# Latent attention on one core: rotation by repeated rows, one table of inverse roots, queries left unnormed until the exponential

## The reference

```python
def pool_mixer(u, pool_w, pool_scale):
    ...
    for g, w in enumerate(POOL_WINDOWS):
        lo = jnp.clip(t - w // 2, 0, S - 1)
        hi = jnp.clip(t + w - 1 - w // 2, 0, S - 1)
        sums = cs[:, hi + 1, g] - cs[:, lo, g]
        cnt = (hi - lo + 1).astype(jnp.float32)[None, :, None]
        outs.append(sums / cnt - ug[:, :, g])
    d = jnp.stack(outs, axis=2).astype(u.dtype)
    y = jnp.einsum('bsgc,gcd->bsgd', d, pool_w).reshape(B, S, POOL_WIDTH)
    return y * pool_scale

def mla_mixer(c_q, c_kv, k_r, q_lora_g, w_uq, kv_lora_g, w_ukv, q_g, k_g):
    q = (rms_norm(c_q, q_lora_g) @ w_uq).reshape(B, S, MLA_HEADS, MLA_QK)
    kv = (rms_norm(c_kv, kv_lora_g) @ w_ukv).reshape(B, S, MLA_HEADS, MLA_NOPE + MLA_V)
    k_nope, v = kv[..., :MLA_NOPE], kv[..., MLA_NOPE:]
    k = jnp.concatenate([k_nope, jnp.broadcast_to(k_r[:, :, None, :], (B, S, MLA_HEADS, MLA_ROPE))], axis=-1)
    q = rms_norm(q, q_g)
    k = rms_norm(k, k_g)
    q = jnp.concatenate([q[..., :MLA_NOPE], rotary(q[..., MLA_NOPE:], pos)], axis=-1)
    k = jnp.concatenate([k[..., :MLA_NOPE], rotary(k[..., MLA_NOPE:], pos)], axis=-1)
    o = blocked_attention(q, k, v)   # softmax over 512 keys, 128 queries at a time
```

## Time and profile before

| | |
|---|---|
| Time, three runs | 3940.98 us median (3920.44 to 3941.12) |
| Profiled execution: its time, its span | 3940.72 us, 3938.9 us |
| TensorE's granted clock, mean | 0.941 |
| PE / DVE / ACT / POOL busy | 93% / 53% / 32% / 3% |
| Length of the changed part: end of `pool[1]` to first matmul of `mix_out[0]` | 150.4 to 396.3 us |

### The profile page before, as it was taken

The page is one execution under the profiler, slowest core; times in us unless marked ns, Lnnn a source line. Parts: engine busy times, 40 slices in busy tenths (PEclk is TensorE's granted clock), DMA queues, the critical chain, the costliest instruction groups (busy, mean ns, idle before and its releaser), DMA issues.

```text
span 3938.9 us, 42380 instructions
## 1 busy us (share of the span) xinstructions
PE 3648.7 (93%) x17470; PEld 2846.9 (72%) x17470; DVE 2083.8 (53%) x3851; ACT 1256.4 (32%) x2098; POOL 111.9 (3%) x216
## 2 busy tenths in 40 slices
PE   7767999999998989999999998999999899889999
PEld 6422767888786768887798566788888786567886
DVE  5665457885665448884314655433333425644444
ACT  4334333333445333333311213332322312224332
POOL 0000000000113000000000000000000000000000
PEclk9878999999999999999999867999999999779999
DMA  5200214552221214552411011122221321112231
GB/s 166 84 0 0 71 48 150 171 171 96 82 70 35 75 43 160 172 171 89 150 54 54 9 46 43 43 65 65 63 67 39 136 65 36 37 46 78 93 97 64
DMA packets 213565, 315.39 MB, mean 80 GB/s; under 512 B 5241, under 2 KB 162555, under 8 KB 212093
## 3 DMA queue, kind: packets, MB, share of 16 engines
q1 hardware_dynamic: 197564, 241.39, 19.0%
q0 software_dynamic: 15808, 71.31, 5.2%
HBM read 300.09 MB, written 14.49 MB: 80 GB/s over the span
## 4 chain that ended last, share of the span: by engine, by line
PE 80%; DVE 13%; ACT 4%; issue 2%; DMA 1%; POOL 0%; SPq 0%; DVEq 0%; POOLq 0%; ACTq 0%
PE ps L94 79%; DVE t L115 5%; ACT t L100 4%; DVE t L107 4%; DVE t L111 1%; PE ps L97 1%; DVE ps L107 1%; DVE ps L115 1%; DVE ps L112 0%; DVE t L112 0%; DVE t L121 0%; DVE t L118 0%; DMA t<-gates_away 0%; DVE t L125 0%; DMA t<-in_mem 0%
## 5 line engine op out<-in xcount | busy, mean ns | idle before, releaser
L94 PE MATMUL ps<-t,t 128*128 128x512 f32 (+7 forms) x16990 | 3557.8, 373 | 258.8 <-DVE t L107 99.9
L94 PEld LDWEIGHTS ps<-t,t 128*128 128x128 f32 (+4 forms) x16990 | 2782.5, 192 | 1008.7 <-issue 223.6
L100 ACT ACTIVATE t<-t 128x1024 fp32r<-128x1024 f32 (+7 forms) x1207 | 853.7, 740 | 1275.9 <-PE ps L94 900.4
L107 DVE TENSOR_TENSOR t<-t,t 128x1024 fp32r<-128x1024 f32 (+5 forms) x884 | 779.1, 906 | 719.0 <-ACT t L100 704.1
L100 ACT ACTIVATE t<-ps 128x512 f32<-128x512 f32 (+6 forms) x481 | 244.4, 530 | 1134.0 <-PE ps L94 1037.5
L115 DVE SCALAR_TENSOR_TENSOR t<-t,t,t 128x256 f32<-128x256 f32 (+4 forms) x951 | 448.4, 535 | 7.6 <-ACT t L100 1.2
L107 DVE TENSOR_TENSOR t<-ps,t 128x512 f32<-128x512 f32 (+4 forms) x308 | 198.1, 663 | 300.7 <-PE ps L94 216.1
L115 DVE SCALAR_TENSOR_TENSOR t<-ps,t,t 128x512 f32<-128x512 f32 (+1 forms) x220 | 133.6, 658 | 279.3 <-PE ps L94 279.1
L118 DVE COPY t<-ps 128x256 f32<-128x256 f32 (+3 forms) x173 | 78.9, 483 | 273.8 <-PE ps L94 255.4
L100 ACT ACTIVATE t<-ps,t 128x512 f32<-128x512 f32 (+3 forms) x153 | 93.7, 617 | 192.5 <-PE ps L94 120.1
L112 DVE TENSOR_SCALAR ps<-ps 128x512 f32<-128x512 f32 (+2 forms) x61 | 39.5, 661 | 110.8 <-ACT t L100 110.8
(11 more groups left out here) (30 smaller groups left out, 304.1 us busy)
## 6 DMA issues: line engine op xcount, KB each, us to landing
t<-in_w_ff SPq DMA_DIRECT2D x64, 1024.0 KB, 7.6
t<-in_w_mlp SPq DMA_DIRECT2D x64, 1024.0 KB, 5.2
t<-in_ada_w POOLq DMA_DIRECT2D x48, 1024.0 KB, 5.7
t<-in_w_in SPq DMA_DIRECT2D x30, 1024.0 KB, 5.3
t<-in_w_qkv_o SPq DMA_DIRECT2D x12, 1024.0 KB, 5.2
t<-in_w_mem_kv SPq DMA_DIRECT2D x8, 1024.0 KB, 6.2
t<-in_w_mem_q SPq DMA_DIRECT2D x8, 1024.0 KB, 5.1
t<-in_w_mem_o SPq DMA_DIRECT2D x8, 1024.0 KB, 5.1
```

What stands on the lines that cost most here:

```text
L94: return Issued(self, self.e and self.e.matmul(o, l, r, start=start, stop=stop, skip_group_check=True))
L100: return Issued(self, self.e and self.e.activation(o, i, f, **kw))
L107: return Issued(self, self.e and self.e.tensor_tensor(o, a, b, op))
```

## The change

Nothing outside the part described above changes but tables: the constants grow by 208 columns (`sel`), and the up-projections are laid out anew on the host.

- Up-projection of queries: the matrix has 128 columns per head: 64 plain, the 32 rotated ones, and the same 32 with halves exchanged. One DVE pass out of PSUM multiplies by gains and by `E0.QROPE` (ones, cosines, sines) and gives `E0.QF`, 128 rows for each head; even heads have the plain rows first, odd heads last. The inverse root of the query is not applied.
- Keys: the shared rotated rows are turned once (a 32-row matmul, three small DVE passes) and copied by four DMAs into both repeated places of all heads of `E0.KX`; ACT copies the plain rows. A score is then one 128-row product.
- Roots: squares of the 12 projection tiles go as stationary operand against 16 columns of `sel`; the sums of 8 queries and 8 keys gather in one bank, [128 tokens, 4x16]. One Ln, one Exp, one Newton step give `E0.RQ` for all. The query's root enters as the per-token scale of the score's exponential (`RQS`, and `NRQ` for the maximum). The key's root is spread over partitions by four 128x128 matmuls against the identity (`key_roots(h)`) and multiplied into `E0.KX` (`keys(h)`), two heads ahead.
- Attention: scores in three banks (0, 1, 2), transposes in 3 and 4. Values for two heads together, on every second turn, with the matmuls of the two heads alternating: one writes rows 0 to 63 of bank 5, the other rows 64 to 127 of bank 7.
- Pools: ACT copies the projected groups out of PSUM into padded rows `E0.R`; the shifted sums, the product and the difference are on GpSimd. `pool_mix` moves into the turns 2 to 5 of attention, its evictions into turns 3 to 6.
- SP: `E0.QROPE` is loaded into a staging buffer, then SP waits for the turned key rows and for `pool[1]`, starts the four copies, and waits for the last query tile before it loads on.

The diff, cut to its core (removed lines are those of the functions above):

```diff
+    E0.M, pt = ar([128, 2, 8, S], R), ar.at
+    E0.WQ, E0.INV = place([128, 2, 1024], F, D1S + 8192), place([128, 4, S], F, D1S + 24576)
+    E0.PT, E0.V = [ar([128, 4, S]) for _ in range(2)], ar([128, 4, 512])
+    E0.R, E0.U, E0.U2 = [ar([128, S + 32]) for _ in range(4)], ar([128, S + 32]), ar([128, S + 32])
+    E0.PW, E0.RQ, E0.RQS, E0.NRQ = ar([128, 4, 128]), ar([128, 64]), ar([128, 64]), ar([128, 64])
+    ar = Area(HRbase := DYN, D1S)
+    E0.QF, E0.KX = ar([128, 8, S]), ar([128, 8, S])
+    spare = U.pool[1].i % 2
+    E0.SB = [place([128, 4, S], F, HLbase[spare] + 8192 * i) for i in range(2)]
+    E0.QROPE = place([128, 2, S], F, STGbase[spare])
...
+        opening(7)
+        pe.wait_ge("krg")
+        pe.matmul(P[7][64:96, :], cst("perm96")[64:96, 64:96], E0.KR[64:96, :], True, True).then_inc("krot")
+        free[7] = [("krt",)]
         feature(U.pool[1], HR1, normed("mix0"))
...
+        def norm_sum(x):
+            kind, n = latent[x]
+            sel = cst("sel")[:, 16 * (n if kind == "q" else 8 + n):][:, 0:16]
+            pe.wait_ge("psq", x)
+            for i in range(4):
+                ins = pe.matmul(P[6][:, 16 * i:16 * i + 16], squares[x % 4][:, 128 * i:128 * i + 128], sel, False, x == 11)
+            ins.then_inc("psum", x)
...
+        pe.wait_ge("krsq")
+        for i in range(4):
+            pe.matmul(P[6][:, 16 * i:16 * i + 16], E0.KSQ[64:96, 128 * i:128 * i + 128], cst("sel")[64:96, 192:208], i == 0, False)
+        for x, (kind, n) in enumerate(latent):
+            bk = latent_banks[x % 6]
+            opening(bk)
+            if kind == "k":
+                pe.matmul(P[bk][:, :], E0.WKV[:, 128 * n:128 * n + 128], E0.CKV[:, :], True, True).then_inc("pk", n)
+                free[bk] = [("psq", x), ("kx", n, 0), ("kx", n, 1)]
+            else:
+                for kk in range(2):
+                    ins = pe.matmul(P[bk][:, :], E0.WQ[:, kk, 128 * n:128 * n + 128], E0.CQ[:, kk, :], kk == 0, kk == 1)
+                ins.then_inc("pq", n)
+                free[bk] = [("psq", x), ("qf", n)]
+            if x > 1:
+                norm_sum(x - 2)
+        norm_sum(10)
+        norm_sum(11)
+        free[6] = [("rs", "mlar")]
+        for i in range(4):
+            bk = latent_banks[i]
+            opening(bk)
+            pe.matmul(P[bk][:, :], E0.CKV[:, 128 * i:128 * i + 128], E0.WKV[:, 512:1024], True, True).then_inc("val", i)
+            free[bk] = [("val_out", i)]
...
+        def key_roots(h):
+
+            opening(6)
+            pe.wait_ge("rs", "mlar")
+            for i in range(4):
+                ins = pe.matmul(P[6][:, 128 * i:128 * i + 128], E0.RQ[:, 16 * i + 8 + h:16 * i + 9 + h].broadcast_to([128, 128]),
+                                cst("ident"), i == 0, i == 3)
+            ins.then_inc("rkb", h)
+            free[6] = [("kf", h)]
...
+            free[6] = [("mixed", m)]
...
+        def transposes(h, kt):
+            bk = 3 + kt % 2
+            opening(bk)
+            for q in range(4):
+                pe.wait_ge("prob", h, q)
+                ins = pe.transpose(P[bk][:, 128 * q:128 * q + 128], E0.SB[h % 2][:, q, 128 * kt:128 * kt + 128], cst("ident"))
+            ins.then_inc("tp", "mla", h, kt)
+            free[bk] = [("pt", h, kt)]
...
+        for h in range(-1, 9):
+            for q in range(4):
+                g = h + 1
+                if g < 8:
+                    bk = (4 * g + q) % 3
+                    opening(bk)
+                    pe.wait_ge("kf", g)
+                    pe.matmul(P[bk][:, :], E0.QF[:, g, 128 * q:128 * q + 128], E0.KX[:, g, :], True, True).then_inc("qk", "mla", g, q)
+                    free[bk] = [("sfree", "mla", g, q)]
+                if q == 0 and h > 0 and h % 2 == 0:
+                    j = h // 2 - 1
+                    opening(5)
+                    opening(7)
+                    for kt in range(4):
+                        for a in range(2):
+                            pe.wait_ge("pt", 2 * j + a, kt)
+                            ins = pe.matmul(P[5 + 2 * a][64 * a:64 * a + 64, :], E0.V[:, kt, 64 * (2 * j + a):64 * (2 * j + a) + 64],
+                                            E0.PT[a][:, kt, :], kt == 0, kt == 3)
+                    ins.then_inc("pv", "mla", j)
+                    free[5], free[7] = [("ol", "mla", j, 0)], [("ol", "mla", j, 1)]
+                if q == 2 and 0 <= h < 6:
+                    key_roots(h + 2)
+                if 0 <= h < 8 and q > 0:
+                    transposes(h, q - 1)
+                if q == 3 and 2 <= h < 6:
+                    pool_mix(h - 2)
+            if 0 <= h < 8:
+                transposes(h, 3)
...
+
+        def pool_in(u):
+            act.wait_ge("pads")
+            for t in u.tiles:
+                act.wait_ge(*ready(u, t))
+                act.activation(E0.R[t.m][:, 16:16 + S], t.views[0].ps, ACT.Copy).then_inc("ev", u.n, t.m, 0)
+
+        pool_in(U.pool[0])
+        pool_in(U.pool[1])
+        for x, (kind, n) in enumerate(latent):
+            ps = P[latent_banks[x % 6]][:, :]
+            act.wait_ge("pk" if kind == "k" else "pq", n)
+            act.wait_ge(*(("psum", x - 4) if x >= 4 else ("hss", "ql", 1) if x < 2 else ("nlo", "mix0", 7, 0)))
+            act.activation(squares[x % 4][:, :], ps, ACT.Square).then_inc("psq", x)
+            if kind == "k":
+                    act.activation(E0.KX[64 * a:64 * a + 64, 2 * n + a, :], ps[64 * a:64 * a + 64, :], ACT.Copy).then_inc("kx", n, a)
+        act.wait_ge("psum", 11)
+        act.activation(E0.RQ[:, :], P[6][:, 0:64], ACT.Ln, bias=EP[:, 0:1], scale=1.0 / 96).then_inc("ln", "mlar")
+        act.wait_ge("ln", "mlar")
+        act.activation(E0.RQ[:, :], E0.RQ[:, :], ACT.Exp, scale=-0.5).then_inc("guess", "mlar")
...
+        def copies(h, kt):
+            act.wait_ge("tp", "mla", h, kt)
+            if h >= 2:
+                act.wait_ge("pv", "mla", h // 2 - 1)
+            act.activation(E0.PT[h % 2][:, kt, :], P[3 + kt % 2][:, :], ACT.Copy).then_inc("pt", h, kt)
...
+                    act.wait_ge("max", "mla", g, q)
+                    act.activation(E0.SB[g % 2][:, q, :], P[(4 * g + q) % 3][:, :], ACT.Exp, bias=st[:, 1:2],
+                                   scale=E0.RQS[:, 16 * q + g:16 * q + g + 1], accum_out=st[:, 2:3]).then_inc("sfree", "mla", g, q)
...
+        for x, (kind, n) in enumerate(latent):
+            if kind == "q":
+                dve.wait_ge("pq", n)
+                dve.wait_ge("psq", x)
+                dve.scalar_tensor_tensor(E0.QF[:, n, :], P[latent_banks[x % 6]][:, :], vec("mlaq_g", n % 2), E0.QROPE[:, n % 2, :],
+                                         ALU.mult, ALU.mult).then_inc("qf", n)
+        newton([("mlar", P[6][:, 0:64], E0.RQ[:, :])], 1.0 / 96)
+        dve.wait_ge("rs", "mlar")
+        dve.tensor_scalar(E0.RQS[:, :], E0.RQ[:, :], 96 ** -0.5, None, ALU.mult).then_inc("rqs")
+        dve.tensor_scalar(E0.NRQ[:, :], E0.RQ[:, :], -(96 ** -0.5), None, ALU.mult).then_inc("nrq")
+
+        def keys(h):
+            dve.wait_ge("kx", h // 2, h % 2)
+            dve.wait_ge("kr_in")
+            dve.wait_ge("rkb", h)
+            dve.scalar_tensor_tensor(E0.KX[:, h, :], E0.KX[:, h, :], vec("mlak_g", h % 2), P[6][:, :], ALU.mult, ALU.mult).then_inc("kf", h)
+
...
+                    dve.tensor_tensor(st[:, 1:2], st[:, 0:1], E0.NRQ[:, 16 * q + g:16 * q + g + 1], ALU.mult).then_inc("max", "mla", g, q)
...
+        pl.wait_ge("mla_weights")
+        for m in range(4):
+            pl.wait_ge("ev", U.pool[m // 2].n, m, 0)
+            a, b, c = E0.R[m], E0.U, E0.U2
+            lo, hi, step = 8, 8 + S + 15, 1
+            pl.wait_ge()
+            pl.tensor_tensor(b[:, lo:hi], a[:, lo - 1:hi - 1], a[:, lo:hi], ALU.add).then_inc()
...
+            pl.wait_ge()
+            pl.tensor_tensor(c[:, 16:16 + S], b[:, 16:16 + S], E0.INV[:, m, :], ALU.mult).then_inc()
+            pl.wait_ge()
+            pl.tensor_tensor(a[:, 16:16 + S], c[:, 16:16 + S], a[:, 16:16 + S], ALU.subtract).then_inc("pooled", m)
...
+        sp.wait_ge("lo", U.pool[1].i, 1)
+        sp.dma_start(E0.QROPE[:, :, :], A["qrope"]).then_inc(s_rope, "qrope")
+        sp.wait_ge("krr")
+        for y, r in enumerate((64, 96, 0, 32)):
+            src = E0.KRR[64:96, :].rearrange("p (a t) -> p a t", a=1).broadcast_to([32, 4, S])
+            ins = sp.dma_start(E0.KX[r:r + 32, y // 2::2, :], src)
...
+        sp.wait_ge("qf", 7)
```

342 lines of the change are left out of this document (143 added, 199 removed).

## The result

| | before | after |
|---|---|---|
| Time, median | 3938.18 us (3920.44 to 3941.12, four runs) | 3808.16 us (3806.64 to 3832.28, four runs) |
| Ratio of after to before | | 0.9694, 95% interval 0.9653 to 0.9735 |
| Profiled execution: its time, its span | 3940.72, 3938.9 us | 3806.64, 3804.9 us |
| Granted clock, mean | 0.941 | 0.952 |

Faster by 3.1%, as forecast: 3808 for 3810 us, inside the range.

What follows compares the result with a forecast made beforehand. TensorE, busy 93% of 3938.9 us, was taken as the bound, with its waits in the changed part to be won; its re-added time line starts the output projection 131 us earlier, so 3940.7 us becomes 3810 us, range 3785 to 3843.

Steps and rivals of the forecast that it cites:

- Step 1: Before the projections: turning the shared key rows once, two TensorE instructions, 0.9 us, to 151.3 us.
- Step 2: Projections and roots: TensorE the bound, small instructions at 0.12 us, 32.6 us in sum, to 183.9 us.
- Step 3: Projections to attention: spreading of roots, DVE's product and two value copies behind the value tiles; first score at 187.1 us.
- Step 4 and 5: Attention turns: 7.2 us without values; 11.3 us with values, ACT the bound, value pair 3.6 us side by side.
- Step 6: Pools in the turns: TensorE 0.86 us more where it waits for ACT anyway; DVE 0.75 more; +0.75 us.
- Step 7: Attention's sum: warming up 5.4, turns 64.6, last transposes and values 8.1 us, from 187.1 to 265.2 us.
- Beside it: Work beside TensorE: GpSimd passes 1.9 to 2.8 us, ending at 176 to 192; DMAs covered; scale column taken at zero.
- (a): Rival, value products: the array's halves take turns, +3.4 us in each of four pairs, 3823 us; chance 0.17.
- (b): Rival, clock: half clock in the projections' part, up to 3843 us; in the turns too, 50 more; chance 0.09.
- (c): Rival, turns: hand-overs as long again, or DVE late by another 2 us each turn, 3826 to 3835 us; chance 0.12.
- (d): Rival, attention: heads still run one after the other, 27.3 us a turn, 3922 us; chance 0.04.
- (e): Rival, pools on GpSimd: each us they end after 215 delays the end by one; 3971 us at 13 a pass; chance 0.03.

Runs made afterwards that it cites:

- e4: Changed kernel with each of the 48 small sum products (16 columns) done twice, the second into an unread bank; 3831.12 us.
- e11: Changed kernel with one extra 512-column float32 product for each of the twelve projection tiles, into an unread bank; 3821.16 us.
- e5: Changed kernel with the 18 pool passes moved back from GpSimd to DVE; 3805.07 us.
- e7: Changed kernel with the four pool products and their evictions moved from the attention turns into the projections; 3813.13 us.
- e8: Changed kernel with five contraction steps of the output projection's first tile pair put into the gaps at the end of attention; 3803.07 us.
- e2: Changed kernel with every GpSimd pool pass done three times, 54 passes in place of 18; 3820.60 us (one execution).
- e1: Changed kernel with the value instructions of a pair's two heads one head after the other instead of alternating; 3824.41 us.
- e3: Changed kernel with every GpSimd pool pass done five times, 90 passes in place of 18; 3861.99 us (one execution).

## Why the prediction was right, point by point

The mechanism was right: TensorE's own work in this order, nearly without waits, sets the time. That the time came within 2 us of the forecast is in part luck. With the turning of the key rows (0.9 us) the changed part takes 116.8 us, 2.0 more than the forecast's 114.8, and inside it terms are off by up to 2 us either way; what lies ahead of it was 1.5 us shorter in this execution than before, and what lies behind it 3.4.

- Step 1. The turning of the shared key rows stands in front of `pool[1]` and its 0.9 us went into the stretch before; the projections begin at 149.8 us, not 151.3. From run to run this start lies between 149.8 and 152.6 us, so that these 1.5 us are luck.
- Step 2, projections and roots. 32.6 us to 183.9 predicted; 149.8 to 182.2 us measured, 32.4, with TensorE busy all the time. A small product with 16 columns costs 0.112 us, against 0.12 from the row of one column; e4 gives the same. Of the bounds 0.10 and 0.43 the first was the near one; by it the sum would have been 2 us less, and not the 10 that the prediction names, which is what all these products cost together. That TensorE is the bound is shown by e11, and e5 shows that DVE is not.
- Step 3. From the first spreading of roots (182.2) to the first score (185.5) 3.3 us, for 3.2.
- Step 4 and 5. Turns 0 to 6: 8.0, 6.7, 11.05, 8.7, 11.9, 8.7, 10.9 us for 7.2, 7.2, 11.3, 8.0, 12.0, 8.0, 10.9. The value pair takes 3.6 us, as taken. ACT's chain behind the values ends turn 2, as forecast, though ACT is busy only 6.4 of its 11.05 us; TensorE with the pool product is as long (above). In a turn without values I had the last division 2.75 us after the start and the scores until 1.7, so 1.05 us of wait; it was 1.0 in turn 0 and 0.4 in turn 1.
- Step 6. The pool product costs nothing in turn 2 (11.05 us, 11.01 in e7) and 0.9 us in turn 4 (11.92, 11.01), near the 0 and 0.75 forecast. In turns 3 and 5 it costs 2.0 each (8.7, and 6.7 in e7) for 0.8: the +0.75 missed that TensorE has nobody to wait for there, so that its 0.86 us come on top of the 0.9 us by which the next head's roots wait for DVE to evict the pool from their bank.
- Step 7. Warming up, from the first score to turn 0, 4.1 for 5.4, the end 10.2 for 8.1: the 16 last transposes and the first values run at half the clock after 3.3 us of waits for ACT, 1.9 and 1.0 us more. In e8, with the gap filled, the clock stays at 1. From the first score on 80.2 us for 78.1; with the start 1.6 us earlier the output projection comes at 265.7 for 265.2.
- Beside it. GpSimd's passes: 1.9 us estimated from shorter ones, 1.06 to 1.28 alone and up to 2.14 beside DVE; the last ends at 165.0 for 176 to 192. The slope of two rows was no guide, one an addition, the other a multiplication by a scalar. The cover in time was larger than said, and worth less (e2). The four key copies and the query table cost nothing that shows: no wait of TensorE names a DMA. The scale column was taken at zero, and that was wrong: the 32 exponentials of attention take 0.778 us each for 0.685 before, 3.0 us of ACT together, the upper end of the "zero to 3 us". Where ACT's chain ends a turn, this is in it; what it costs the kernel was not run. The 32 passes of before, then of after:

```profile
L100 ACT ACTIVATE t<-ps,t 128x512 f32<-128x512 f32 x32 | 21.9, 685 | 35.9 <-DVE t L111 35.8
```

```profile
L100 ACT ACTIVATE t<-ps,t,t 128x512 f32<-128x512 f32 x32 | 24.9, 778 | 29.1 <-DVE t L107 29.1
```

- The rivals. (a) fell: side by side, e1. (b) happened for 2.9 us at the end alone, and turns with 16 transposes each stayed at 1.00; e4 shows how it comes in the projections, and I had argued only from idle time. (c) fell: TensorE waits 9.9 us in all. (d) fell: turns of 6.7 and 11 us. (e) did not decide: e3 bears out its price, e2 moves its threshold.
- 131 us were forecast as the earlier start of the output projection and 130.6 came, 129.1 of them in the changed part.

## What to carry to other kernels

Where engines wait for each other in a chain of short steps per head, work that does not depend on the head's order (projections, squares, one table of roots) belongs in front, in a stage where TensorE alone is the bound; the time can then be added up from TensorE's rows, within 2 us here. A part that relieves an engine may be worth nothing once another part has taken that engine off the path: take it back alone before crediting it. And an engine without a gap need not be the one that ends a stage: take work off it and see whether the stage gets shorter. Last, fill the end of a pipeline with the first steps of what comes next: it saves the gap and the half clock behind it.

## What the runs showed of the hardware

- TensorE's clock fell to half with TensorE busy all of the 28 us ahead and waiting for nobody, when each group of 16-column products stood twice (157 instructions in that time); with nearly the same time in 512-column products (117 instructions) it stayed at 1.
- TensorE starts a product in one column half of the array ahead of products queued before it for the other half; this is read from the spacing of the starts in e1, whose rows do not name the halves: with the two heads one after the other, 12 steps of 0.43 us instead of 8 or 16. The Trainium skill (TensorE: Matmul & The Clock Gate, Part 3: Packing small matmuls — row/col tiling, The mechanism) says that products start strictly in the order of the program; e1's rows speak against that for the two halves.
- DVE and GpSimd at work on SBUF together: on the mean, a division pass goes from 0.49 to 1.40 us (e2), a product of two 512-column operands from 0.71 to 1.5 (e5, after), a 128x1 product from 0.16 to 0.44 (e2); passes with one operand in PSUM, or with no operand but PSUM, are unchanged. GpSimd's addition of 527 columns goes from 1.06 to 1.9 us (after).
- An exponential of 128x512 out of PSUM on ACT takes 0.685 us with a scale that is a number (before) and 0.778 with a column of scales (after).
